# Moving the RMS statistics of four normalisations to one value per token in a fused two-block transformer kernel

## The reference

```python
def rms_norm(x, w):
    xf = x.astype(jnp.float32)
    y = xf * lax.rsqrt(jnp.mean(xf * xf, axis=-1, keepdims=True) + EPS)
    return (y * w.astype(jnp.float32)).astype(x.dtype)

for l in range(DEPTH):                       # DEPTH = 2
    with_ctx_out = l < DEPTH - 1
    h_lat = rms_norm(x, norm_pre_mix[l]) * (1.0 + sc1) + sh1
    h_ctx = rms_norm(ctx, norm_pre_mix[l]) * (1.0 + sc1c) + sh1c
    ...                                      # l = 0: attention and HGRN2; l = 1: neighbourhood attention
    x = x + g1 * rms_norm(y_lat, norm_post_mix[l])
    h_lat = rms_norm(x, norm_pre_ffn[l]) * (1.0 + sc2) + sh2
    x = x + g2 * rms_norm(conv_ffn(h_lat, ...), norm_post_ffn[l])
    if with_ctx_out:
        ...                                  # the same for ctx

# in gqa_axial_attention, before the rotary embedding
q_lat, q_ctx = rms_norm(q_lat, q_norm_w), rms_norm(q_ctx, q_norm_w)
k_lat, k_ctx = rms_norm(k_lat, k_norm_w), rms_norm(k_ctx, k_norm_w)
```

## Time and profile before

| | |
|---|---|
| time of three runs, us | 2607.11, 2608.29, 2614.7 (median 2608.29) |
| the profiled execution, us | 2608.29 |
| its span, us | 2606.5 |
| granted TensorE clock, mean over the span | 0.948 of full speed |
| busy: PE, PEld, DVE, ACT, POOL | 91%, 79%, 51%, 43%, 5% |
| the four calls start at (us of the span) | 1276.5, 1723.1, 2123.9, 2379.6 |
| first work of the phase after each | 1295.1, 1741.7, 2157.5, 2392.4 |

### The profile page before, as it was taken

The page is one execution under the profiler, slowest core; times in us unless marked ns, Lnnn a source line. Parts: engine busy times, 40 slices in busy tenths (PEclk is TensorE's granted clock), DMA queues, the critical chain, the costliest instruction groups (busy, mean ns, idle before and its releaser), DMA issues. The chain is left out here.

```text
span 2606.5 us, 42008 instructions
## 1 busy us (share of the span) xinstructions
PE 2384.1 (91%) x16464; PEld 2046.7 (79%) x16464; DVE 1321.7 (51%) x2140; ACT 1131.1 (43%) x1986; POOL 130.9 (5%) x169
## 2 busy tenths in 40 slices
PE   7998998999999899999788998769999988986998
PEld 6887977888888787888556887648888777865997
DVE  5443246444544315644554666565555554436665
ACT  3333244443434325443346666424443444434554
POOL 1000001000100000100000222100000000001000
PEclk9999989999999979999899999889999988988999
DMA  7876124885787521588311111124344252304663
GB/s 226 258 249 192 35 65 124 238 257 157 223 255 243 150 60 54 154 257 251 115 40 41 45 55 42 34 69 129 109 121 121 99 144 81 90 1 131 188 178 92
DMA packets 394139, 350.09 MB, mean 134 GB/s; under 512 B 24228, under 2 KB 357400, under 8 KB 393496
## 3 DMA queue, kind: packets, MB, share of 16 engines
q1 hardware_dynamic: 383924, 297.61, 39.8%
q10 hardware_dynamic: 10084, 50.66, 5.4%
HBM read 347.18 MB, written 1.05 MB: 134 GB/s over the span
## 5 line engine op out<-in xcount | busy, mean ns | idle before, releaser
L547 PE MATMUL ps<-x_hi,gu_hi 128*128 128x256 f32 x1680 | 478.4, 285 | 0.0
L547 PE MATMUL ps<-x_lo,gu_hi 128*128 128x256 f32 x1680 | 475.4, 283 | 0.0
L547 PE MATMUL ps<-x_hi,gu_lo 128*128 128x256 f32 x1680 | 475.4, 283 | 0.0
L547 PEld LDWEIGHTS ps<-x_hi,gu_hi 128*128 128x128 f32 x1680 | 321.9, 192 | 22.7 <-DVE gu_lo L692 17.5
L547 PEld LDWEIGHTS ps<-x_lo,gu_hi 128*128 128x128 f32 x1680 | 322.2, 192 | 2.6
L547 PEld LDWEIGHTS ps<-x_hi,gu_lo 128*128 128x128 f32 x1680 | 322.2, 192 | 0.0
L692 DVE TENSOR_TENSOR gu_lo<-w_gu,gu_hi 128x1024 fp32r<-128x1024 f32 x220 | 266.8, 1249 | 87.3 <-ACT gu_hi L623 87.3
L623 ACT ACTIVATE gu_hi<-w_gu 128x1024 fp32r<-128x1024 f32 x220 | 221.9, 1051 | 47.6 <-issue 30.0
L634 ACT ACTIVATE silu<-ps 128x256 f32<-128x256 f32 x88 | 33.8, 384 | 416.2 <-PE ps L547 404.2
L718 DVE SCALAR_TENSOR_TENSOR hid<-silu,ps 128x256 f32<-128x256 f32 x88 | 37.0, 421 | 316.5 <-ACT silu L634 316.5
L573 PE MATMUL ps<-dn_hi,h_hi 128*128 128x512 f32 x440 | 173.7, 395 | 7.2 <-DVE h_lo L727 7.2
(11 more groups left out here) (416 smaller groups left out, 5161.4 us busy)
## 6 DMA issues: line engine op xcount, KB each, us to landing
w_gu<-in_ffn_w_up SPq DMA_DIRECT2D x178, 512.0 KB, 6.2
w_dn<-in_ffn_w_down SPq DMA_DIRECT2D x134, 512.0 KB, 3.8
w_mod<-in_w_mod ACTq DMA_DIRECT2D x64, 768.0 KB, 6.3
w_gu<-in_ffn_w_gate SPq DMA_DIRECT2D x90, 512.0 KB, 5.2
odd_w<-in_odd_w_qkv SPq DMA_DIRECT2D x24, 512.0 KB, 5.2
w_gu<-in_ffn_w_down SPq DMA_DIRECT2D x11, 1024.0 KB, 5.0
hgrn_w<-in_even_w_in SPq DMA_DIRECT2D x20, 512.0 KB, 3.9
w_in_q<-in_w_in SPq DMA_DIRECT2D x2, 3072.0 KB, 11.7
```

Source lines behind the costliest of these rows:

```text
L547: last = pe.matmul(gu(n)[:, a, :], wt[n][:, a, f, :], x[:, f, :], start=(f == 0 and p == 0), stop=(f == FT - 1 and p == 2), skip_group_che ...
```

## The change

In `prenorm_phase` ScalarE now squares six tiles and VectorE two. All eight squares are added up elementwise, two of the adds on GpSimd and five on VectorE. TensorE then takes the summed squares as weights, 128 tokens at a time, with one column of ones as the moving operand (`eps[:, 2:3]`, which holds 1): the sums come out with the tokens on the partitions, one value per token, 128 x 4 in all. Root and reciprocal work on that. VectorE then makes a diagonal matrix of each 128 values, and TensorE multiplies it with the matrix of ones, which puts r for each token on all partitions, now in PSUM bank 1. The product h reads r from there. In the third call bank 1 of the bias products is made between the two groups of matmuls and the banks 2 to 12 after the second. In `gqa_project` the gains of all ten heads are loaded side by side, and one instruction multiplies them in.

```diff
-    ALONE, ADDED, OWN = (0, 1, 2), (3, 4), (5, 6, 7)
+    NT = n // P
+    BY_ACT = (2, 3, 0, 1, 5, 4)
...
-        total, std, r = sq[:, 5, :], sq[:, 6, :], sq[:, 7, :]
+        std, r = sb("pre_std", [P, NT]), sb("pre_r", [P, NT])
+        diag = sb("pre_diag", [P, NT, P])
...
-                for f in ALONE + ADDED:
+                for f in BY_ACT:
                     act.activation(sq[:, f, :], k.x_T[:, f, c0:c0 + n], ACT.Square).then_inc(s["sq_done"], 1)
-                    if bias and f == 0:
+                    if bias and f == BY_ACT[0]:
                         bias.keep_turned(act, k, s)
                 act.wait_ge(s["sum_done"], 1)
-                act.activation(std, k.ps[:, 0, 0:n], ACT.Sqrt, bias=k.eps[:, 1:2], scale=1.0 / D).then_inc(s["std_done"], 1)
+                act.activation(std[:, :], k.ps[:, 0, 0:NT], ACT.Sqrt, bias=k.eps[:, 1:2], scale=1.0 / D).then_inc(s["std_done"], 1)
...
+                pool.wait_ge(s["sq_done"], 2)
+                pool.tensor_tensor(sq[:, 2, :], sq[:, 2, :], sq[:, 3, :], ALU.add).then_inc(s["side_step"], 1)
+                pool.wait_ge(s["sq_done"], 5)
+                pool.wait_ge(s["side_step"], 1)
+                pool.tensor_tensor(sq[:, 2, :], sq[:, 2, :], sq[:, 5, :], ALU.add).then_inc(s["side_step"], 1)
...
-                for f in ALONE:
-                    pe.wait_ge(s["sq_done"], f + 1)
-                    pe.matmul(k.ps[:, 0, 0:n], k.ones[:, :], sq[:, f, :], start=(f == 0), stop=False)
                 pe.wait_ge(s["acc_done"], 1)
-                pe.matmul(k.ps[:, 0, 0:n], k.ones[:, :], total, start=False, stop=True).then_inc(s["sum_done"], 1)
+                for tt in range(NT):
+                    last = pe.matmul(k.ps[:, 0, tt:tt + 1], sq[:, 6, tt * P:(tt + 1) * P], k.eps[:, 2:3], start=True, stop=True,
+                                     skip_group_check=True)
+                last.then_inc(s["sum_done"], 1)
                 if bias:
-                    bias.products(pe, k, s, range(1, Bias.BANKS))
+                    bias.products(pe, k, s, range(1, 2))
+                pe.wait_ge(s["diag_done"], NT)
+                for tt in range(NT):
+                    last = pe.matmul(k.ps[:, 1, tt * P:(tt + 1) * P], k.ones[:, :], diag[:, tt, :], start=True, stop=True, skip_group_check=True)
+                last.then_inc(s["spread"], 1)
+                if bias:
+                    bias.products(pe, k, s, range(2, Bias.BANKS))
...
-                for f in OWN:
+                for f in (6, 7):
                     last = dve.tensor_tensor(sq[:, f, :], k.x_T[:, f, c0:c0 + n], k.x_T[:, f, c0:c0 + n], ALU.mult)
                 c.link(last)
-                for f in OWN[1:]:
-                    c.link(dve.tensor_tensor(total, total, sq[:, f, :], ALU.add))
-                for f in ADDED:
-                    dve.wait_ge(s["sq_done"], f + 1)
-                    last = dve.tensor_tensor(total, total, sq[:, f, :], ALU.add)
...
+                c.link(dve.tensor_tensor(sq[:, 6, :], sq[:, 6, :], sq[:, 7, :], ALU.add))
+                for f, made in ((0, 3), (1, 4), (4, 6)):
+                    dve.wait_ge(s["sq_done"], made)
+                    c.link(dve.tensor_tensor(sq[:, 6, :], sq[:, 6, :], sq[:, f, :], ALU.add))
+                dve.wait_ge(s["side_step"], 2)
+                dve.tensor_tensor(sq[:, 6, :], sq[:, 6, :], sq[:, 2, :], ALU.add).then_inc(s["acc_done"], 1)
...
-                dve.reciprocal(r, std).then_inc(s["r_done"], 1)
+                dve.reciprocal(r[:, :], std[:, :]).then_inc(s["r_done"], 1)
                 dve.wait_ge(s["r_done"], 1)
+                for tt in range(NT):
+                    dve.tensor_scalar(diag[:, tt, :], k.ident[:, :], r[:, tt:tt + 1], None, ALU.mult).then_inc(s["diag_done"], 1)
+                dve.wait_ge(s["spread"], 1)
...
-                        dve.tensor_tensor(b.h_T[:, f, c0:c0 + n], k.x_T[:, f, c0:c0 + n], r, ALU.mult).then_inc(s["n_done"], 1)
+                        dve.tensor_tensor(b.h_T[:, f, c0:c0 + n], k.x_T[:, f, c0:c0 + n], k.ps[:, 1, 0:n], ALU.mult).then_inc(s["n_done"], 1)
...
-    m.gain = sb("qk_gain", [P, 2, HD2])
+    m.gain = sb("qk_gain", [P, GQ + GKV, HD2])
...
-    for n, name in enumerate(("even_q_norm_2", "even_k_norm_2")):
-        loads.append((m.gain[:, n, :], w[name].broadcast_to([P, HD2])))
+    for h in range(GQ + GKV):
+        g = w["even_q_norm_2"] if h < GQ else w["even_k_norm_2"]
+        loads.append((m.gain[:, h, :], g.broadcast_to([P, HD2])))
...
-                    for h0, n, g in ((0, GQ, 0), (GQ, GKV, 1)):
-                        last = dve.tensor_tensor(qk[:, h0:h0 + n, :], qk[:, h0:h0 + n, :], m.gain[:, g, :].unsqueeze(1).broadcast_to([P, n, HD2]), ALU.mult)
-                    c.link(last)
+                    c.link(dve.tensor_tensor(qk, qk, m.gain[:, :, :], ALU.mult))
```

More of the change, by code:

```diff
@@ L1628, in prenorm_phase @@
 def prenorm_phase(nc, k, b, l, ffn, streams, ahead=(), first=False, bias=None):
-    names = ["sq_done", "acc_step", "acc_done", "sum_done", "std_done", "r_done", "scaled", "n_done", "ahead_in"]
+    names = ["sq_done", "side_step", "acc_step", "acc_done", "sum_done", "std_done", "r_done", "diag_done", "spread", "scaled", "n_done", "ahead_in"]
     names += Bias.SEMS if bias else []
     c0, n = streams[0] * S, len(streams) * S
-    ALONE, ADDED, OWN = (0, 1, 2), (3, 4), (5, 6, 7)
+    NT = n // P
+    BY_ACT = (2, 3, 0, 1, 5, 4)
     with ExitStack() as ctx:
@@ L1700, in _ @@
                 c = Chain(dve, s["acc_step"])
-                for f in OWN:
+                for f in (6, 7):
                     last = dve.tensor_tensor(sq[:, f, :], k.x_T[:, f, c0:c0 + n], k.x_T[:, f, c0:c0 + n], ALU.mult)
                 c.link(last)
-                for f in OWN[1:]:
-                    c.link(dve.tensor_tensor(total, total, sq[:, f, :], ALU.add))
-                for f in ADDED:
-                    dve.wait_ge(s["sq_done"], f + 1)
-                    last = dve.tensor_tensor(total, total, sq[:, f, :], ALU.add)
-                    if f != ADDED[-1]:
-                        c.link(last)
-                last.then_inc(s["acc_done"], 1)
+                c.link(dve.tensor_tensor(sq[:, 6, :], sq[:, 6, :], sq[:, 7, :], ALU.add))
[4 more added lines that the diff above has]
+                dve.tensor_tensor(sq[:, 6, :], sq[:, 6, :], sq[:, 2, :], ALU.add).then_inc(s["acc_done"], 1)
                 if first:
```

## The result

The changed kernel takes **2624.73 us** (median of 8 runs, 2615.09 to 2629.07) where the kernel before takes 2608.67 in the runs beside it. The ratio is 1.0056, 95% interval 1.0039 to 1.0073: slower by 10.2 to 19.0 us. The forecast of 2617.5 has the sign, but the time lies above its range. The profiled execution took 2618.02 (span 2615.9).

The account below looks back on a forecast made before the run. It took most of the kernel as matmul-bound (TensorE busy 91%), the change touching four short phases where TensorE mostly waits. 2.7 + 2.7 + 3.9 + 0 - 0.1 = 9.2 on 2608.29 gave 2617.5 us, range 2609 to 2622.

Parts of the forecast that it names:

- Gains: Gain loads and multiplication for the projection: one multiplication saves 0.1 in all, eight more loads stay hidden under other work.
- if that cover were gone: Case in which no work hides the eight added gain loads: they would cost 1 to 2 us.
- GpSimd's adds: Two adds beside VectorE's chain: each keeps VectorE out for 1.08 us, 2.16 together; half width in N4, 1.1.
- rival of free adds: GpSimd's adds cost nothing: 2.16 off N1 and N2, 2.0 off N3, giving 2611.2; chance 0.14.
- Sum, root, reciprocal, diagonals, spread: Chain from accumulation to h in N1: 1.9, 0.29, 0.18, 0.9, 1.9, with hops 5.5 us, where now 5.39.
- N1: Normalisation phase before the first mixer: forecast 2.7 us longer, h 2.4 later.
- N2: Normalisation phase before the two-stream feed-forward: forecast 2.7 us longer, with the same sums as N1.
- rival in which the reciprocal's saving shows in full: Sum and spread at full clock, GpSimd free: N1 and N2 -0.9 each, N3 -5.6, giving 2600.8; chance 0.03.
- h from PSUM: Product h reading r from PSUM: 0.05 more an instruction, 0.3 us in N1 (bounds 0 and 0.6).
- N3: Phase before the neighbourhood attention, with the bias table: products queue behind the spread at half clock, 3.9 us longer.
- full-clock rival: TensorE runs N3's bias products at full clock, phase 5.6 us sooner: 2608.0, no slower; chance 0.11.
- N4: Last, one-stream phase: compute ends 1.4 later, inside the 1.7 that a weight load leaves; term 0.

Follow-up runs that it names:

- after: The changed kernel itself, against the kernel before: 2624.73 us, ratio 1.0056.
- e1: The changed kernel with its gains part undone (two gain loads, two multiplications), new normalisation kept: 2614.85 us, +0.26% against the kernel before.
- e2: The kernel before with only the gains part of the change (ten loads, one multiplication): slower by 0.20%.
- e5: The changed kernel with its ten gain loads reading 128 different rows of another constant, so the gains are wrong: 2623.13 us.
- e3: The changed kernel with its ten gain loads issued as two DMAs writing the same bytes: N1 lasts 23.76 us.
- e4: The changed kernel with the first call's small loads ahead of the 3072 KB weight load: N1 lasts 28.71 us.
- e6: The kernel of e1 with GpSimd's two adds done by VectorE: 2625.20 us in its only run; N1 lasts 20.23 us.
- e7: The kernel of e1 with the third call in the form of the kernel before: 2619.20 us, +0.32% against the kernel before.
- e12: The kernel of e7 run once more, beside a repeat of e1: 2614.99 us, interval 1.0007 to 1.0029.
- e8: The kernel of e1 with four wide matmuls on TensorE before the third call's sum: N3 lasts 33.88 us; the ratio's low end is 1.0022.

## Why the prediction was wrong, and where it was right

**The step that failed** is *Gains*: "0.9 us by size and perhaps twice that by their short rows, so done by 1289, under work that ends past 1295". I priced the loads by bytes. The ten gain loads, cosine and sine needed 14.1 us after the big load had landed (1287.4 to 1301.5), not under 2. Both covers ran out: compute ended at 1297.8, the phase at 1301.9. The same sentences had the right question ("if that cover were gone") and a wrong price for it, 1 to 2. The term was -0.1 and measured +3.8 (after less e1), or +5.1 by itself (e2).

The row I had the earlier trace rows shows the big load alone. The two gain loads of before would have misled as well: they land 0.2 to 0.4 us behind the big one. A hint stood elsewhere in the trace of before:

```profile
hgrn_gain<-in_hgrn_out_norm SPq DMA_DIRECT2D x1, 64.0 KB, 6.7
```

```profile
1352.00:1353.00 1.00, 0.00 (x0) 0.00 (x0) 0.98 (x1) 1.00 (x3) 0.00 (x0) 1.00 0.36 70
```

This load, issued at 1347.40, spreads one 512-byte row over 128 partitions, and just before it lands the queue moves only 70 GB/s, with loads of 512 KB waiting behind it. That it is this load which slows the queue there is a reading that no run isolates.

The cause of the 3.8 us is that the ten loads read the same two rows over and over (e5), not issue time (after, e5), number of issues (e3) or order (e4). What makes such reads start so rarely is not shown. The Trainium skill, DMA: Bandwidth & Descriptors, section Why a DMA increments its semaphore by 16 and not by 1, lets the slowest dimension decide how many engines a load uses, and for 128 partitions that is all sixteen. The trace agrees: after has, beside the data, 208 packets of 4 bytes between the first issue and the last landing, sixteen for each of its 13 loads and as many as each load adds to its semaphore, and e5 has 208 too. The share of 0.07 is thus not one engine of sixteen at full work.

**GpSimd's adds** went as forecast, in mechanism and nearly in size. The accumulation ended at 1284.24, 6.9 after the phase's start, where the working gave 7.07. The two stretched adds lost 0.99 and about 0.95 against the 1.08 each that I took from the earlier trace rows. The rival of free adds is excluded by e6, where VectorE alone is faster.

**Sum, root, reciprocal, diagonals, spread** measured 1.86, 0.27, 0.18, 0.87 and 2.07 against 1.9, 0.29, 0.18, 0.9 and 1.9. First h came 12.40 after N1's start and 12.38 after N2's; 12.6 was forecast. The rival in which the reciprocal's saving shows in full is out: 3.17 us less of reciprocal are spent on the narrow chain at half clock.

**h from PSUM** was the other mis-sized term: 0.3 forecast, 0 measured (two products in 1.28, as the 1.29 from SBUF in the earlier trace rows). So the compute part of N1 and N2 is +2.19 and +2.15, not +2.7 each.

**N3** is +4.11 against +3.9, with its mechanism: products at 0.216 a record, clock 0.50 to the end. How near the number came is partly luck: against the old form in e2, e7 and e12 it is 3.1 to 3.3. The full-clock rival needed the products to raise the clock by themselves, and in 23 us without a gap they did not. e8 shows that it was the wide matmuls that were missed. **N4** is +0.2 against 0, which is within its scatter; its h comes 1.08 later, as forecast (1.1), and its load still ends it.

So the forecast of 9.2 becomes 2.15 + 2.15 + 4.1 + 0.2 + 3.8 = 12.4. The measured medians differ by 16.1, and the other 3.7 are within the interval and not explained. The range was too narrow as well: its upper end had no case for late loads, although eight DMAs were added to a phase that must wait for all of them.

## What to carry to other kernels

Price an added load by its access pattern and its number and not by its bytes: two loads of a kind that cost nothing do not say what ten of them cost, and what lands under a big load has no price in its row. When an engine's work is made "smaller", ask what the old work did for others: here a wide matmul kept the clock up for the products behind it. Work moved to GpSimd as a helper costs VectorE about 1 us for each 128x512 add that runs beside its own.

## What the runs showed of the hardware

- Ten loads one after the other that each spread one 256-byte row over 128 partitions (32 KB each, eight from one row and two from another) move at 17 to 35 GB/s with a DMA share of 0.07 to 0.15; the same size from 128 different rows costs nothing that shows (e5), and neither do two such loads behind a big one (before). A 3072 KB load queued behind the ten lands after 22.7 us instead of 10.1 (e4).
- 64x96 products in a row stay at a granted clock of 0.50 for over 20 us without a gap, and after four wide matmuls, under which the clock rose to 1.00, it falls back to 0.50 under the same products without a pause (e8).
- A one-column float32 matmul costs as much as one of 96 columns at half clock: 0.43 from start to start, where each loads its own weights. Narrowing below that buys nothing here.
- A 128x512 two-input VectorE product costs the same with one input in PSUM as with both in SBUF (1.28 and 1.29 for two).
